# Neighbourhood attention on one Trainium2 core: from 64 units of one grid row to 32 units of 8x16 queries and 12x32 keys

## The reference, cut to what matters

```python
col_start = jnp.clip(cols - kc // 2, 0, GRID_W - kc)        # kc = 16, GRID_W = 64
rs = jnp.clip(r - kr // 2, 0, rows - kr)                    # kr = 8, rows = 16
s = einsum('bwhd,brwjhd->bhwrj', q_r, k_win) * scale + bias  # 8 x 16 keys per query
p = softmax(s over the 128 keys)
out = einsum('bhwrj,brwjhd->bwhd', p, v_win)
```

## Time and profile before

| | |
|---|---|
| median of three runs | 1843.69 us |
| the profiled execution's own time | 1837.65 us |
| its span, first to last instruction | 1835.9 us |
| TensorE busy, products / weight loads | 1629.6 us (89%) / 1179.3 us (64%) |
| VectorE, ScalarE, GpSimd busy | 724.1 us (39%), 510.9 us (28%), 509.0 us (28%) |
| attention stage, last V transpose of pair 0 to last L850 | 274.00 to 578.71 us |

### The profile page before, as it was taken

The page is one execution under the profiler, slowest core; times in us unless marked ns, Lnnn a source line. Parts: engine busy times, 40 slices in busy tenths (PEclk is TensorE's granted clock), DMA queues, the critical chain, the costliest instruction groups (busy, mean ns, idle before and its releaser), DMA issues.

```text
span 1835.9 us, 37277 instructions
## 1 busy us (share of the span) xinstructions
PE 1629.6 (89%) x14820; PEld 1179.3 (64%) x14820; DVE 724.1 (39%) x1319; ACT 510.9 (28%) x902; POOL 509.0 (28%) x472
## 2 busy tenths in 40 slices
PE   2799999999998999999998994399999989999960
PEld 1677786777766787787886883155555555555630
DVE  1745536565656334435223756011111111111118
ACT  1456534444455112111002210022222222222214
POOL 4522221111113332333331210432333323232332
PEclk8899999999999999999999995699999999999985
DMA  9541010101001433443122316579999999979836
GB/s 311 164 141 33 24 46 24 35 24 30 17 12 41 124 99 97 126 143 98 51 80 105 100 40 266 206 274 399 400 400 401 400 400 402 400 300 397 327 116 223
DMA packets 178855, 333.88 MB, mean 182 GB/s; under 512 B 38382, under 2 KB 100470, under 8 KB 178750
## 3 DMA queue, kind: packets, MB, share of 16 engines
q1 hardware_dynamic: 145774, 272.59, 40.2%
q0 software_dynamic: 24256, 42.96, 7.0%
q10 hardware_dynamic: 8720, 16.80, 3.0%
HBM read 302.44 MB, written 29.72 MB: 181 GB/s over the span
## 4 chain that ended last, share of the span: by engine, by line
PE 55%; DVE 7%; DMA 3%; issue 2%; POOL 1%; ACT 0%; DVEq 0%; SPq 0%; ACTq 0%; POOLq 0%
PE ps L950 18%; PE ps L711 13%; PE ps L961 9%; PE ps L879 7%; PE ps L904 5%; PE ps L940 1%; DMA w_exp<-in_w_exp_up 1%; DVE act L1613 1%; PE ps L911 1%; POOL d_list L614 1%; DVE br_lo L1440 1%; DMA ada_g<-in_ada_w 1%; DVE res L1646 1%; DVE y L1636 1%; DVE x L1637 1%
## 5 line engine op out<-in xcount | busy, mean ns | idle before, releaser
L950 PE MATMUL ps<-w_exp,xT 128*32 128x256 f32 x6272 | 350.9, 382 | 4.5 <-DMA w_exp<-in_w_exp_up 4.5
L711 PE MATMUL ps<-u_hi,w_hi 128*128 128x512 f32 x768 | 312.6, 407 | 0.9 <-ACT lx L1035 0.9
L711 PE MATMUL ps<-u_lo,w_hi 128*128 128x512 f32 x768 | 305.7, 398 | 0.0
L711 PE MATMUL ps<-u_hi,w_lo 128*128 128x512 f32 x768 | 300.8, 392 | 0.0
L950 PEld LDWEIGHTS ps<-w_exp,xT 128*32 128x32 f32 x6272 | 208.0, 111 | 138.6 <-issue 8.6
L541 POOL CAST w_hi<-w_raw 128x1024 fp32r<-128x1024 f32 x48 | 60.8, 1267 | 571.2 <-issue 335.0
L961 PE MATMUL ps<-w_exp,actT 128*32 128x256 f32 x3136 | 179.5, 381 | 0.0
L1613 DVE TENSOR_TENSOR act<-act,ps 64x256 f32<-64x256 f32 x98 | 41.6, 424 | 342.6 <-ACT act L1203 341.1
L711 PEld LDWEIGHTS ps<-u_hi,w_hi 128*128 128x128 f32 x768 | 145.1, 189 | 36.2 <-issue 9.4
L711 PEld LDWEIGHTS ps<-u_hi,w_lo 128*128 128x128 f32 x768 | 144.9, 189 | 28.6
L711 PEld LDWEIGHTS ps<-u_lo,w_hi 128*128 128x128 f32 x768 | 145.3, 189 | 25.1 <-issue 1.0
(11 more groups left out here) (254 smaller groups left out, 2277.9 us busy)
## 6 DMA issues: line engine op xcount, KB each, us to landing
w_exp<-in_w_exp_gate SPq DMA_DIRECT2D x32, 2048.0 KB, 27.0
w_exp<-in_w_exp_up SPq DMA_DIRECT2D x32, 2048.0 KB, 26.6
w_exp<-in_w_exp_down SPq DMA_DIRECT2D x32, 2048.0 KB, 27.0
ada_g<-in_ada_w ACTq DMA_DIRECT2D x32, 512.0 KB, 3.8
d_y<-yb POOLq DMA_DIRECT2D x98, 128.0 KB, 7.3
w_raw<-in_w_in SPq DMA_DIRECT2D x24, 512.0 KB, 4.1
w_raw<-in_w_branch_gate SPq DMA_DIRECT2D x24, 512.0 KB, 4.1
ada<-in_ada_w SPq DMA_DIRECT2D x4, 2048.0 KB, 15.0
```

What stands on the lines that cost most here:

```text
L711: ins = pe.matmul(ps[:, 5 + h, :], a[par][:, kc, :], b[:, kc, HF[h]], start=(n == 1), stop=(n == MM))
L950: last = pe.matmul(ps[CAP * n:CAP * (n + 1), 2 + h, 0:QT], x, w[n // 2][:, off:off + QT], start=(kc == 0), stop=(kc == KC - 1))
```

## The change

A unit becomes a block of 8 rows by 16 columns of queries, for both heads of the pair, and its keys are the 12 rows by 32 columns that these queries can reach: 384 keys for each head. There are 8 units in a pair, 32 in all. Per unit:

- **Scores** (L882): two products of 384 columns, one for each head, with the 64 features of the head as the contraction: head 0 on array rows 0 to 63, head 1 on rows 64 to 127, into two PSUM banks. `q_bd` and its copies are gone; ScalarE now writes Q in the units' order.
- **Softmax** on VectorE and ScalarE is done for each head on 128x384, and the probabilities are scaled by the reciprocal sum ahead of the transposes (L1473); before, the output was.
- **Transposes** (L917): six for a unit.
- **All eighteen fill products** stand between transposes and value products.
- **Values** (L928): six products of 128 columns; the head's 64 values are the stationary columns, head 0 on array columns 0 to 63 and head 1 on columns 64 to 127. The output comes out with features in the partitions, so L850 is gone, and one copy takes it to `y_na` (L1213).
- **Bias**: GpSimd builds a table of shifted and column-masked rows for all heads (two times three additions, L612), SyncE's queue stores it to HBM in eight transfers, and 24 sets of 128x768 are loaded from it into a ring of three (two transfers each), where GpSimd adds a row mask (L623).
- **Order**: K's job now comes ahead of Q's; in the last of the first jobs the V transposes and the first scores stand after 6 of 24 products. V is evacuated in two operations. A half of a job that ends in the second half of a unit's fill is evacuated after the unit's output copy.

```diff
+QR, QC = 8, 16
+KR, KW = 12, 32
+KEYS = KR * KW
+KT = KEYS // P
+CBLK = GRID_W // QC
+UNITS = ROWS // QR * CBLK
+COL0 = (0, 8, 24, 32)
+KIND = (0, 1, 1, 2)
+KINDS = 3
+SETS = ROWS // QR * KINDS
+PADR = NREL + 2 * (QR - 1) - 6
...
+def place(u):
+
+    hp, r = divmod(u, UNITS)
+    return (hp,) + divmod(r, CBLK)
+
+
+def bias_set(u):
+
+    hp, half, c = place(u)
+    return (hp * 2 + half) * KINDS + KIND[c]
+
+
+def last_unit(n):
+
...
-        vtok = at("vtok", 148, [P, 2, 15, P])
-        bias = at("bias", 163, [P, 2, NREL * GRID_W])
-        window = at("window", 170.5, [P, GRID_W])
+        vT = at("vT", 100, [P, CBLK, ROWS, KW])
...
+        prob = at("prob", 144, [P, 2, 2, KEYS])
+        probT = at("probT", 150, [P, 2, KT, P])
+        vtok = at("vtok", 153, [P, 2, 4 * CBLK, P])
+        bias = at("bias", 195, [P, 3, 2, KEYS])
...
+        VT0 = 3
...
+        SHARE = 2 * MM * PER // UNITS
+        SBANK, TBANK, YBANK = (0, 2), (3, 4), 7
+
+        def finish_at(i, h):
+
+            u, n = divmod(MM * (2 * i + h + 1) - 1, SHARE)
+            return u, n // (SHARE // 2)
 
...
+            def store_table(g):
+
+                sp.wait_ge(table_set, g + 1)
+                for i in range(4):
+                    dst = d_table.ap()[4 * g + i].rearrange("k i r c -> r (k i) c")
+                    sp.dma_start(dst, table[i * PADR:(i + 1) * PADR]).then_inc(st_table, 16)
+
+            def load_bias(n):
+
+                if n >= 3:
+                    sp.wait_ge(s_biased, 2 * (last_unit(n - 3) + 1))
+                hp, half, kind = n // SETS, n // KINDS % 2, n % KINDS
                 for side in range(2):
-                    src = bass.AP(d_rpb, ((2 * hp + side) * NREL) * RPAD, [[1, GRID_W], [RPAD, NREL], [1, GRID_W]])
-                    dst = bias[64 * side:64 * side + 64, hp % 2, :].rearrange("p (r c) -> p r c", r=NREL)
-                    sp.dma_start(dst, src).then_inc(ld_bias, 16)
+                    first = (((2 * hp + side) * KINDS + kind) * QC * PADR + 4 * (1 - half)) * KW
...
+            sp.wait_ge(f_done, 4)
+            for h in range(2):
+                sp.wait_ge(st_y[h], 16)
+            sp.wait_ge(st_table, 16 * HEADS)
+            for n in range(3):
+                load_bias(n)
+            load_job(PRO + 2, *jobs[2])
             for hp in range(PAIRS):
-                for i, job in enumerate(FILL[hp]):
-                    load_job(PRO + PER * hp + i, *job)
-                if hp == PAIRS - 1:
-                    break
-                sp.wait_ge(bias_ready, hp + 1)
-                if hp:
-                    sp.wait_ge(s_biased, done(ROWS * hp - 1))
-                else:
-                    sp.wait_ge(f_done, 4)
-                load_bias(hp + 1)
+                n, i = SETS * hp, PER * (hp + 1)
+                more = hp < PAIRS - 1
+                load_bias(n + 3)
+                if more:
+                    load_job(PRO + i, *jobs[i])
+                load_bias(n + 4)
...
+            def build_table(g):
+
+                if g:
+                    pool.wait_ge(st_table, 16 * 4)
+                for kind in range(KINDS):
+                    v = rpb_pad[:, g, QC - 8 * kind:QC - 8 * kind + KW]
+                    shifted = bass.AP(v.tensor, v.offset, [v.ap[0], [1, QC], [1, KW]])
+                    own = slice(kind * QC, (kind + 1) * QC)
+                    ins = pool.tensor_tensor(table[:, own, :], shifted, colmask[:, own, :], ADD)
+                    if kind == KINDS - 1:
+                        ins.then_inc(table_set, 1)
+                    else:
+                        ch.mark(ins)
+
+            def mask_bias(n):
+
+                pool.wait_ge(ld_bias[n % 3], 32 * (n // 3 + 1))
+                b3 = bias[:, n % 3].rearrange("p h (r c) -> p (h r) c", c=KW)
+                rows = rowmask[:, n // KINDS % 2, :].unsqueeze(2).to_broadcast([P, 2 * KR, KW])
+                pool.tensor_tensor(b3, b3, rows, ADD).then_inc(bias_ready, 1)
...
+                n, k = SETS * hp, PRO + PER * hp
+                mask_bias(n + 3)
+                mask_bias(n + 4)
+                split_job(k + 2)
+                mask_bias(n + 5)
                 if hp < PAIRS - 1:
-                    mask_bias((hp + 1) % 2, hp * 32 + 64)
+                    mask_bias(n + 6)
+                    split_job(k + 3)
+                    mask_bias(n + 7)
+                    mask_bias(n + 8)
+                    split_job(k + 4)
...
+            def scores(u):
+
+                hp, half, c = place(u)
+                if c == 0:
+                    pe.wait_ge(job_evac, 2 * (PRO + PER * hp) - 1 + half)
+                pe.wait_ge(s_biased, 2 * u)
+                for h in range(2):
+                    own = slice(DH * h, DH * (h + 1))
+                    keys = cells(kT[own, hp % 2])[:, 4 * half:4 * half + KR, COL0[c]:COL0[c] + KW]
+                    pe.matmul(ps[:, SBANK[h], 0:KEYS], qT[own, hp % 2, half, c, :], keys, start=True, stop=True).then_inc(s_ps, 1)
+
...
+            last_job = job_half_mms(PRO - 1, (PRO - 1) % 2, 1, PRO, 2 * (PRO - 1))
+            run(last_job, MM // 4)
+            pe.wait_ge(vt_evac, 3)
+            transpose_v(3)
+            scores(0)
+            run(last_job)
...
-                for r in range(ROWS):
-                    u = hp * ROWS + r
-                    if r < ROWS - 1:
-                        scores(par, r + 1, u + 1)
-                    elif more:
-                        scores(nxt, 0, u + 1)
-
-                    pe.wait_ge(p_ready, done(u))
-                    pe.wait_ge(pt_ready, done(u - 2))
-                    for i in range(4):
-                        last = pe.transpose(ps[:, 2 + 5 * (r % 2), i * P:(i + 1) * P], prob[r % 2][:, i * P:(i + 1) * P], ident[:])
-                    last.then_inc(pt_ps, 1)
-                    run(fg, share // 2)
-
-                    pe.wait_ge(pt_ready, done(u))
-                    pe.wait_ge(o_ready, done(u - 1))
-                    t0 = band(r) // 2 if band(r) % 2 == 0 else 8 + band(r) // 2
-                    for i in range(4):
-                        rhs = vtok[:, par, t0 + i, :]
-                        last = pe.matmul(ps[:, 3, 0:P], probT[r % 2][:, i, :], rhs, start=(i == 0), stop=(i == 3))
+                for r in range(UNITS):
+                    u = hp * UNITS + r
+                    _, half, c = place(u)
+                    if u + 1 < PAIRS * UNITS:
+                        scores(u + 1)
+
+                    pe.wait_ge(pt_ready, 2 * u)
+                    for h in range(2):
+                        pe.wait_ge(p_ready, 2 * u + h + 1)
+                        for i in range(KT):
+                            last = pe.transpose(ps[:, TBANK[h], i * P:(i + 1) * P], prob[:, u % 2, h, i * P:(i + 1) * P], ident[:])
+                        last.then_inc(pt_ps, 1)
+                    run(fg, SHARE)
+
+                    pe.wait_ge(pt_ready, 2 * u + 2)
+                    if u >= 2:
+                        pe.wait_ge(y_ready, u - 1)
+                    cols = slice(u % 2 * P, (u % 2 + 1) * P)
+                    for i in range(KT):
+                        for h in range(2):
+                            own = slice(DH * h, DH * (h + 1))
+                            last = pe.matmul(ps[own, YBANK, cols], vtok[:, hp % 2, (half + i) * CBLK + c, own], probT[:, h, i, :],
+                                             start=(i == 0), stop=(i == KT - 1))
                     last.then_inc(o_ps, 1)
-                    run(fg, share - share // 2)
-
-                    pe.wait_ge(o_ready, done(u))
-                    pe.wait_ge(y_ready, done(u - 1))
-                    pe.transpose(ps[:, 4, 0:P], o_bd[r % 2][:], ident[:]).then_inc(ot_ps, 1)
-
                     if more and VT0 <= r < VT0 + 4:
...
+            def exps(u):
+                for h in range(2):
+                    sc.wait_ge(s_biased, 2 * u + h + 1)
+                    p = prob[:, u % 2, h, :]
+                    sc.activation(p, p, ACT.Exp, bias=nmax[:, u % 2, h:h + 1], accum_out=rsum[:, u % 2, h:h + 1]).then_inc(p_exp, 1)
...
+                    if u:
+                        sc.wait_ge(o_ps, u)
+                    for h in range(2):
+                        sc.wait_ge(pt_ps, 2 * u + h + 1)
+                        sc.activation(probT[:, h].rearrange("p a b -> p (a b)"), ps[:, TBANK[h], 0:KEYS], ACT.Copy).then_inc(pt_ready, 1)
+                    if u + 1 < PAIRS * UNITS:
+                        exps(u + 1)
+
+                    def finished(part):
+                        for i in range(PER):
+                            for h in range(2):
+                                if finish_at(i, h) == (r, part):
+                                    evac(PRO + PER * hp + i, h, *FILL[hp][i], (hp + 1) % 2)
+                    finished(0)
+                    sc.wait_ge(o_ps, u + 1)
                     hold(sc)
-                    for side in range(2):
-                        sl = slice(64 * side, 64 * side + 64)
```

(43 more changed lines are left out.)

232 lines of the change are left out of this document (90 added, 142 removed).

## The result

The changed kernel takes 1816.89 us (median of four runs, 1815.17 to 1817.15) beside 1843.63 us for the kernel before on the same chip: a ratio of 0.985 (95% interval 0.9833 to 0.9867), 26.7 us less. The prediction was 84.6 us less and a range of 1745 to 1785: the direction was right, two thirds of the gain are missing.

A forecast was written before the change was run, and what follows sets the result against it. TensorE's list was taken to bound the attention stage (98% busy): 98.0 us saved less give-backs leaves 84.6, so the profiled 1837.65 becomes 1753.0, or 1759.1 against the median; range 1745 to 1785, inner 1746 to 1772.

The forecast's parts named there:

- Ahead of the recurrence: Before the attention stage: three table additions (3.6 us) replace a 2.26 us mask addition, moving VectorE's chain to `xc`; +1.4 us.
- Bias sets, at nothing: Bias loads in the attention stage: a set's slot falls free some 19 us ahead of need, mask 1.8 us; no cost.
- The rival that ended slower: Bias ring: three sets served one after another, 13.5 us each with mask, make the kernel some 1870 us; chance 0.03.
- Scores and values in pairs: TensorE, each unit: the two heads' products overlap on array halves, scores taking 0.64 us and values 0.63.
- Both pairing rivals: Scores or values do not overlap, +20 us, 1779, chance 0.12; both serial, 1799, chance 0.05.
- the rival in which records start in order: TensorE passes start only with or behind their predecessor: scores 0.96 us, values 0.74, +13 us, 1773; chance 0.09.
- Changes of shape: TensorE, each unit: three switches between full array, row halves and column halves, 0.10 us each.
- Start, +4.7: Attention stage's start: unit 0's softmax behind Q's second evacuation delays transposes 3.1 us, then low clock costs 1.6.
- Q's evacuation, +3.3: Next pair's first scores wait for ScalarE's output copy and Q evacuation, 1.1 us, three times.
- Softmax round trip at nothing: Each unit: 4.0 us from scores to scaled probabilities, covered by fill as TensorE returns after 6.28; slack 2.3 us.
- GpSimd in VectorE's way, +2: Attention stage: GpSimd may hold VectorE's new scaling up to 2.4 us, just passing the slack; +2 us.
- End, +1.0: Attention stage's end: ScalarE begins the branch preparation 4.5 us behind the last fill product, where it was 3.5.

The follow-up runs named there:

- e1: Changed kernel with 24 rows in place of 23 in each head's part of the table, nothing else: 1757.36 us, 0.957 of before.
- e12: Kernel with 24 table rows, run again on one chip beside the changed kernel: 1763.72 us, 0.9556 of before.
- e11: Changed kernel as it is, run again on one chip beside the kernel with 24 table rows: 1816.55 us, 0.9842 of before.
- e8: Against the kernel with 24 rows: second head's scores computed from the first head's features, both on the same array half; 1781.10 us.
- both orders: Kernel with 24 rows plus unit 0's exponentials ahead of the last Q evacuation and finished jobs' evacuations ahead of a unit's output copy: 1750.3 us.
- e13: Changed kernel, 23 rows and stores in place, but GpSimd builds the second table behind the split of job 5: 1823.84 us.

## Why the prediction was wrong

**The step that failed** is the last sentence of the term "Ahead of the recurrence": "The second table stands between splits with time to spare, and the zero-fill and stores are needed long after." With it falls the last sentence of "Bias sets, at nothing", that the queue's job loads wait for splits a job ahead. When a store's data are needed was answered rightly, and it was the wrong question. I asked who waits for the stores and not what stands behind them in SyncE's queue: the loads of jobs 5 and 6. I gave the eight stores no duration at all; no row of before shows a transfer like them, and neither end of a range was named. Taken at the nearest row, 7.3 us for 240 KB, eight stores of 138 KB would have been 34 us in sum and still too little; their shape, 1104 pieces on a prime number of rows, was the warning. Measured: 100.1 us of the queue, 53 us of the kernel. The rival that ended slower had the transfers wrong too: it feared the bias loads, and those cost nothing.

**With the stores repaired the sum comes out nearly as forecast.** With 24 rows the medians differ by 79.8 us in e1 and 82.5 in e12, and the profiled spans by 81.0, where 84.6 were predicted; 0.957 and 0.956 against 1759.1 / 1843.69 = 0.954. Part of this is luck, as the terms show:

- *Scores and values in pairs:* right. The scores take 0.84 with their change of shape (0.64 + 0.20), the values 0.81 (0.63 + 0.18). Both pairing rivals fall. So does the rival in which records start in order: it asked for 0.96 without the change, and the records start in twos. The Trainium skill's rule of starts and ends strictly in order (TensorE: Matmul & The Clock Gate, The mechanism) is not borne out for these passes on other rows.
- *Changes of shape:* mis-sized. Behind the fill product's 0.09 the prediction had 3 x 0.10; the unit shows 0.20 ahead of the row halves, 0.10 and 0.18 ahead of and in the column halves, and 0.09 behind the row halves, 0.57 in sum. 32 x 0.27 = 8.6 us more. The divided fill measured the same by itself, 0.26 for one more return to the full array.
- *V transposes:* a unit with them takes 7.17 us, 0.62 more and not 0.45: 2 us in twelve.
- *Start, +4.7:* right in kind. 3.14 and 0.67 us of waiting for L1473, and nine products at 0.43 us behind it, 1.8 us more than at full clock: 5.6. A longer second scaling is in it (1.45 us for 0.42, while GpSimd worked beside it; that this is the reason is not shown).
- *Q's evacuation, +3.3:* the waits were there, released by L1129, in the units named, but 0.36 us each, 1.1 in sum.
- *Softmax round trip at nothing:* right; L917 waited once more, 0.4 us. *GpSimd in VectorE's way, +2*, and *Gelu, +1:* too much. The scaling L1473 reached 2.36 us once and mostly took 0.42; in the steady window above TensorE is busy for 210.27 of 211.77 us.
- *End, +1.0:* the branch preparation began 552.19 - 549.08 = 3.1 us behind the last fill product and not 4.5, as the Gelu table had been loaded at 544.64. The first product of the gates came 21.2 us behind it, where it was 19.4 (597.86 - 578.44): 1.8.
- *Recurrence, +1.4:* TensorE's wait for `xc` did not grow. It was 2.3 us in the first profile of the changed kernel and 0.5 in its second (e11), 0.5 in e1 and 2.3 in e8, both with 24 rows, against 2.45. So it goes with the execution, and why is not settled. Behind 0.5 the eight products L829 took 3.70 us at a granted clock of 1.00, behind 2.45 before 5.40 at 0.76. In e1 these two make 3.6 of the 4.7 us by which the first L882 (266.5) came sooner than computed (269.8 + 1.4). The forecast has no merit in them.
- *Bias sets at nothing:* right. A mask takes 1.49 us and not 1.8, and no L882 or L917 waited for one.

Added up, shape, V transposes, start and end took 12.3 us more than forecast; Q, GpSimd and Gelu took 4.8 less, and the first scores came 4.7 sooner: 84.6 - 12.3 + 4.8 + 4.7 = 81.8 us, where the first product of the gates came 81.0 sooner in e1. Misses on both sides cancel to within 4 us. The inner range does not follow from its own terms either: 9.6 for the shapes and 7 for the waits, each to either side, give 1742.5 to 1775.7 and not 1746 to 1772.

## What to carry to other kernels

Price every new transfer by its shape and by what stands behind it in its queue, not only by who reads it: bytes said 34 us, the queue was held for 100. An outer dimension that is prime (23) can put a whole transfer on one engine; one row of padding or a split in 16 + 7 gave the 53 us back, and so did spacing the stores between the loads. When a large gain does not appear, look first at where the changed stage begins: it was as short as forecast, and only 50 us late.

An evacuation that waits for a long job costs what stands behind it, not its own 0.6 us: the exponentials put ahead of it made the first units 6.6 us shorter, and with 24 rows and both orders the kernel takes 1750.3 us, 0.951 of before.

## What was not expected of the hardware

- 128-byte pieces of a 23-row store went out every 11.6 ns, at 11 GB/s; with 24 rows of the same pieces four stores moved at 138 GB/s, and the median issue took 0.73 us and not 12.94.
- 23 rows in pieces of 6 KB moved at 27 GB/s with 6.5% of 16 engines, and did not hold the queue.
- A store that is slow does not hold the queue itself: alone it was issued in 0.74 us, and the next transfer was held for 13.8 us.
- Beside the 8 MB zero-fill the queue stood 7.8 and 16.1 us at two 7-row stores, where the 16-row stores between them took 1.7 to 1.8.
- Products of two heads on different row halves of the array ran wholly beside one another (0.84 us for both, 1.48 on the same half).
- The experts' stage took 591.0 to 594.9 us in eleven profiles and 599.5 to 600.5 in four (after, e11, e12, e13), for unchanged code and at the same granted clock; chip number 14 had both lengths.
